# Opening loads reordered, first two units by halves, a wide form for gate and up, and new places for small vector work in a two-layer encoder trunk

## The reference, cut to what matters

```
x   : (1, 256, 1024)
# layer 0
h   = x @ e_w_in                       # 1024 x 2312: q, k, v of two head groups, forget gates
mix = concat(window_attention(h), forgetting_attention(h)) @ e_w_out
x   = layer_norm(ALPHA * x + mix)
x   = layer_norm(ALPHA * x + (silu(x @ w_gate) * (x @ w_up)) @ w_down)    # hidden width 2816
# layer 1
x   = layer_norm(ALPHA * x + differential_attention(x @ o_w_in) @ o_w_out)
logits = x @ w_router                  # 8 experts, top 2 of 8 for each token
x   = layer_norm(ALPHA * x + sum over the 2 chosen e of gate_e * expert_e(x))   # SwiGLU, hidden width 3584
```

## Time and profile before

| | |
|---|---|
| median of 3 runs | 1441.7 us (1440.79 to 1446.67) |
| the profiled execution | 1441.19 us, span 1439.4 us |
| TensorE busy | 1400.8 us, 97% of the span, 7602 matmuls |
| VectorE busy | 1114.2 us, 77% |
| ScalarE busy | 942.6 us, 65% |
| granted TensorE clock | 0.994 |
| read from HBM | 431.54 MB, 304 GB/s over the span |

### The profile page before, as it was taken

How to read it: one execution, slowest core, us unless ns; L and a number is a source line. 1 busy time by engine, 2 the same in 40 slices (tenths; PEclk the granted TensorE clock), 3 DMA queues, 4 the chain that set the end, 5 groups by cost and what they waited for, 6 DMA issues and landing times.

```text
span 1439.4 us, 19952 instructions
## 1 busy us (share of the span) xinstructions
PE 1400.8 (97%) x7602; PEld 1205.1 (84%) x7602; DVE 1114.2 (77%) x980; ACT 942.6 (65%) x837; POOL 36.7 (3%) x29
## 2 busy tenths in 40 slices
PE   8999999999989999999999999999999999999986
PEld 8988999989978888888888888888888888888865
DVE  4646544565567888988888888888888888889977
ACT  4655434345554777777777777777777777778755
POOL 1000000000000000000000000000000000000200
PEclk9999999999999999999999999999999999999999
DMA  9515545544146999999999999999999999999950
GB/s 364 222 64 215 190 176 189 191 147 176 60 180 260 415 422 379 366 390 386 352 400 382 356 382 386 372 371 385 376 361 411 373 357 389 385 378 374 370 202 31
DMA packets 62789, 438.59 MB, mean 305 GB/s; under 512 B 7096, under 2 KB 7120, under 8 KB 11152
## 3 DMA queue, kind: packets, MB, share of 16 engines
q1 hardware_dynamic: 59904, 425.75, 76.6%
q0 software_dynamic: 2688, 11.85, 2.3%
q10 hardware_dynamic: 144, 0.27, 0.1%
HBM read 431.54 MB, written 6.30 MB: 304 GB/s over the span
## 4 chain that ended last, share of the span: by engine, by line
PE 90%; DVE 4%; ACT 2%; DMA 2%; issue 1%; POOL 0%; SPq 0%; DVEq 0%; POOLq 0%; ACTq 0%
PE ps L503 29%; PE ps L505 28%; PE ps L504 28%; PE ps L873 2%; DMA work<-y_rows,mx 1%; ACT raw L1007 1%; DMA raw<-w_dense 1%; DVE raw L1266 1%; DVE wlo L1238 1%; PE ps L661 1%; PE ps L609 1%; PE ps L510 1%; PE ps L831 0%; DVE raw L1307 0%; DVE biasb L1484 0%
## 5 line engine op out<-in xcount | busy, mean ns | idle before, releaser
L1238 DVE TENSOR_TENSOR wlo<-raw,whi 128x2048 fp32r<-128x2048 f32 x398 | 909.8, 2291 | 203.4 <-ACT whi L957 201.7
L957 ACT ACTIVATE whi<-raw 128x2048 fp32r<-128x2048 f32 x398 | 762.1, 1918 | 274.3 <-PE ps L505 271.9
L503 PE MATMUL ps<-whi,xth 128*128 128x512 f32 (+1 forms) x1144 | 440.8, 385 | 3.3 <-ACT xth L972 1.6
L505 PE MATMUL ps<-whi,xtl 128*128 128x512 f32 (+1 forms) x1144 | 434.3, 380 | 0.0
L504 PE MATMUL ps<-wlo,xth 128*128 128x512 f32 (+1 forms) x1144 | 433.6, 379 | 0.0
L503 PEld LDWEIGHTS ps<-whi,xth 128*128 128x128 f32 x1144 | 215.3, 188 | 46.1 <-DVE wlo L1238 2.6
L505 PEld LDWEIGHTS ps<-whi,xtl 128*128 128x128 f32 x1144 | 215.2, 188 | 41.3
L504 PEld LDWEIGHTS ps<-wlo,xth 128*128 128x128 f32 x1144 | 215.5, 188 | 38.4
L503 PE MATMUL ps<-whi,hth 128*128 128x512 f32 x464 | 183.3, 395 | 7.1 <-DVE wlo L1238 7.1
L504 PE MATMUL ps<-wlo,hth 128*128 128x512 f32 x464 | 181.4, 391 | 0.0
L505 PE MATMUL ps<-whi,htl 128*128 128x512 f32 x464 | 181.4, 391 | 0.0
(11 more groups left out here) (234 smaller groups left out, 678.6 us busy)
## 6 DMA issues: line engine op xcount, KB each, us to landing
raw<-w_moe SPq DMA_DIRECT2D x336, 1024.0 KB, 7.1
raw<-w_dense SPq DMA_DIRECT2D x62, 1024.0 KB, 4.8
raw<-vec_rows POOLq DMA_DIRECT2D x4, 1024.0 KB, 6.1
y_rows<-work SPq DMA_DIRECT2D x8, 512.0 KB, 8.7
x<-x_in SPq DMA_DIRECT2D x2, 512.0 KB, 5.2
raw<-w_dense SPq DMA_DIRECT2D x2, 512.0 KB, 10.0
raw<-cum_rows POOLq DMA_DIRECT2D x1, 1024.0 KB, 9.9
x_rows<-x SPq DMA_DIRECT2D x2, 512.0 KB, 3.0
```

The source lines that it names most:

```text
L503: mm(o, lh, rh, start=start, stop=False)
L505: return mm(o, ll, rh, start=False, stop=stop)
L957: A(unit(whi, j), raw[:, slot * UNIT:(slot + 1) * UNIT], ACT.Copy).then_inc(hi_rdy, 1)
L1238: dve.tensor_tensor(unit(wlo, j), raw[:, slot * UNIT:(slot + 1) * UNIT], unit(whi, j).bitcast(F32), ALU.subtract).then_inc(lo_rdy, 1)
```

## The change

1. SP loads x block 0, first half of unit 0, x block 1, second half of unit 0, then unit 1 in two halves.
2. TensorE transposes only block 0 before unit 0. `first_cols` runs unit 0 by halves: k-tiles 0 to 3 for block 0, then the transposes of block 1, k-tiles 0 to 3 for block 1, then k-tiles 4 to 7 for both. `second_rows` runs unit 1 by halves. ScalarE and VectorE split units 0 and 1 by halves, ScalarE with the eviction of block 1 between the halves of unit 0.
3. `xth` and `xtl` become one tile `xt` with both parts of a k-tile side by side. `to_rows_wide` replaces `to_rows` for gate and up units: high weights times both parts in one matmul of 512 columns, low weights times the high part in one of 256, into a bank for each block. ScalarE copies the second half of each bank to SBUF, VectorE adds the first half to it; silu and product then work from SBUF. Gate uses banks 0 and 1, up banks 2 and 3, without alternation, and TensorE waits for the sum of the chunk before.
4. In `even_end` the evictions and the head output of group 3 stand ahead of the split of unit 12.
5. Ten warm matmuls in the routing become four.
6. `ROWS_AT` and `PICK_AT` have new values.

```diff
-WARM_ROUTE = (8, 8, 10, 3, 8)
+WARM_ROUTE = (8, 8, 4, 3, 8)
-PICK_AT = (24, 27, 30, 33)
-ROWS_AT = (1, 3, 6, 8, 12, 14, 18)
+PICK_AT = (26, 29, 32, 35)
+ROWS_AT = (0, 2, 4, 6, 8, 10, 12)
-        xth = sb("xth", [P, KT, TOK], F32R)
-        xtl = sb("xtl", [P, KT, TOK], F32R)
+        xt = sb("xt", [P, KT, 2, TOK], F32R)
+        xth, xtl = xt[:, :, 0, :], xt[:, :, 1, :]
+        gate_sum = htmp[:, :].rearrange("p (k n) -> p k n", k=2)
+        up_sum = work[:, 256:768].rearrange("p (k n) -> p k n", k=2)
...
-            for tb in range(TB):
-                sp.dma_start(x[:, tb, :], x_in[0, tb * P:(tb + 1) * P, :]).then_inc(x_here[tb], 16)
-            sp.dma_start(raw[:, 0:UNIT // 2], w_dense[0][:, 0:UNIT // 2]).then_inc(first_in, 16)
+            sp.dma_start(x[:, 0, :], x_in[0, 0:P, :]).then_inc(x_here[0], 16)
+            sp.dma_start(raw[:, 0:UNIT // 2], w_dense[0][:, 0:UNIT // 2]).then_inc(first_in[0], 16)
+            sp.dma_start(x[:, 1, :], x_in[0, P:2 * P, :]).then_inc(x_here[1], 16)
             sp.dma_start(raw[:, UNIT // 2:UNIT], w_dense[0][:, UNIT // 2:UNIT]).then_inc(loaded[0], 16)
-            for k in range(1, N_DENSE):
+            sp.dma_start(raw[:, UNIT:UNIT + UNIT // 2], w_dense[1][:, 0:UNIT // 2]).then_inc(first_in[1], 16)
+            sp.dma_start(raw[:, UNIT + UNIT // 2:2 * UNIT], w_dense[1][:, UNIT // 2:UNIT]).then_inc(loaded[1], 16)
+            for k in range(2, N_DENSE):
...
+            def to_rows_wide(k, bank):
+
+                h, l = as_cols(whi, k), as_cols(wlo, k)
+                for b in range(2):
+                    for kt in range(KT):
+                        c = slice(b * P, b * P + P)
+                        mm(ps[bank + b][:, :], h[:, kt, c], xt[:, kt, :, :], start=kt == 0, stop=False)
+                        r = mm(ps[bank + b][:, 0:TOK], l[:, kt, c], xth[:, kt, :], start=False, stop=kt == KT - 1)
+                return r
+
+            def first_cols():
+
+                h, l = as_cols(whi, 0), as_cols(wlo, 0)
+                pe.wait_ge(first_lo, 1)
+                for half in range(2):
+                    if half == 1:
+                        pe.wait_ge(lo_rdy, 1)
+                    for tb in range(TB):
+                        if half == 0 and tb == 1:
+                            turn(0, (2, 3))
+                        for kt in range(4 * half, 4 * half + 4):
+                            t = slice(tb * P, tb * P + P)
+                            r = three(ps[4][:, tb * 256:tb * 256 + 256], xth[:, kt, t], xtl[:, kt, t],
+                                      h[:, kt, :], l[:, kt, :], tb == 0 and kt == 0, tb == 1 and kt == KT - 1)
+                return r
...
-            turn(0)
+            turn(0, (0, 1))
...
-                    if what == "gate" and c >= 2:
-                        pe.wait_ge(f_h, c - 1)
-                    r = to_rows(k, (0 if what == "gate" else 2) + c % 2)
+                    if c:
+                        pe.wait_ge(f_gate if what == "gate" else f_up, c)
+                    r = to_rows_wide(k, 0 if what == "gate" else 2)
...
                 exps(3)
+                probs_out(3)
                 split(U_IN_E - 1 + SPLIT_AHEAD)
-                probs_out(3)
...
-            turned(0)
-            act.wait_ge(first_in, 16)
+            turned(0, (0, 1))
+            act.wait_ge(first_in[0], 16)
             A(whi[:, 0, 0:UNIT // 2], raw[:, 0:UNIT // 2], ACT.Copy).then_inc(first_hi, 1)
+            turned(0, (2, 3))
             act.wait_ge(loaded[0], 16)
             A(whi[:, 0, UNIT // 2:UNIT], raw[:, UNIT // 2:UNIT], ACT.Copy).then_inc(hi_rdy, 1)
...
+                    if what == "gate":
+                        act.wait_ge(w_used, k + 1)
+                        if c:
+                            act.wait_ge(f_lo, c)
+                        for b in range(2):
+                            A(gate_sum[:, b, :], ps[b][:, TOK:], ACT.Copy).then_inc(f_part, 1)
+                        act.wait_ge(f_gate, c + 1)
+                        A(htmp[:, :], htmp[:, :], ACT.Silu).then_inc(f_silu, 1)
                     if what == "up":
                         act.wait_ge(w_used, k + 1)
                         if c:
-                            act.wait_ge(f_lo, c)
-                        A(htmp[:, :], ps[c % 2][:, :], ACT.Silu).then_inc(f_silu, 1)
+                            act.wait_ge(f_h, c)
+                        for b in range(2):
+                            A(up_sum[:, b, :], ps[2 + b][:, TOK:], ACT.Copy).then_inc(f_part, 1)
...
+                    if what != "down":
+                        n0, o, done = (0, gate_sum, f_gate) if what == "gate" else (2, up_sum, f_up)
+                        for b in range(2):
+                            dve.wait_ge(f_part, 4 * c + n0 + b + 1)
+                            r = dve.tensor_tensor(o[:, b, :], ps[n0 + b][:, 0:TOK], o[:, b, :], ALU.add)
+                        r.then_inc(done, 1)
                     if what == "up":
+                        dve.wait_ge(f_up, c + 1)
                         dve.wait_ge(f_silu, c + 1)
-                        dve.tensor_tensor(htmp[:, :], htmp[:, :], ps[2 + c % 2][:, :], ALU.mult).then_inc(f_h, 1)
+                        dve.tensor_tensor(gate_sum, gate_sum, up_sum, ALU.mult).then_inc(f_h, 1)
```

More of the change, by code:

```diff
@@ L195, in hidden @@
             if c < FC - 1:
-                return hth[:, :], htl[:, :]
-            return (t[:, 0:2, :].rearrange("p k n -> p (k n)") for t in (xth, xtl))
+                return [t[:, :].rearrange("p (k n) -> p k n", k=2) for t in (hth, htl)]
+            return xth[:, 0:2, :], xtl[:, 0:2, :]
         cum_t = biasb[0:8, 0, 0:TOK]
@@ L241, in trunk @@
         loaded = [sem(f"loaded{i}") for i in range(SLOTS)]
-        first_in = sem("first_half_unit_in")
-        first_hi = sem("first_half_unit_hi_ready")
-        first_lo = sem("first_half_unit_lo_ready")
+        first_in = [sem(f"first_half_of_unit{k}_in") for k in range(2)]
+        first_hi = sem("first_halves_of_units_hi_ready")
+        first_lo = sem("first_halves_of_units_lo_ready")
         c_in = sem("consts_in")
@@ L285, in trunk @@
         sum_rdy = sem("branch_sum_ready")
+        f_part = sem("ffn_low_part_copied")
+        f_gate = sem("ffn_gate_sum_ready")
+        f_up = sem("ffn_up_sum_ready")
         f_silu = sem("ffn_silu")
@@ L561, in to_cols, with second_rows @@
                                   h[:, kt, 0:n], l[:, kt, 0:n], kt == 0, kt == KT - 1)
+                return r
[12 more added lines that the diff above has]
+                                      h[:, kt, :], l[:, kt, :], tb == 0 and kt == 0, tb == 1 and kt == KT - 1)
+                return r
+            def second_rows():
+                h, l = as_cols(whi, 1), as_cols(wlo, 1)
+                pe.wait_ge(first_lo, 2)
+                for half in range(2):
+                    if half == 1:
+                        pe.wait_ge(lo_rdy, 2)
+                    for b in range(2):
+                        for kt in range(4 * half, 4 * half + 4):
+                            c = slice(b * P, b * P + P)
+                            r = three(ps[5][:, b * TOK:(b + 1) * TOK], h[:, kt, c], l[:, kt, c],
+                                      xth[:, kt, :], xtl[:, kt, :], b == 0 and kt == 0, b == 1 and kt == KT - 1)
                 return r
@@ L572, in project @@
                         pe.wait_ge(in_ev, seen + i - 1)
-                    if k == 0:
-                        pe.wait_ge(first_lo, 1)
-                    else:
+                    if k > 1:
                         pe.wait_ge(lo_rdy, k + 1)
-                    r = to_cols(k, 4 + i % 2, width) if width else to_rows(k, 4 + i % 2)
+                    r = first_cols() if k == 0 else second_rows() if k == 1 else to_cols(k, 4 + i % 2, width) if width else to_rows(k, 4 + i % 2)
                     r.then_inc(w_used, 1)
@@ L1104, in _ @@
                         act.wait_ge(f_h, n + 1)
-                        A(list(hidden(n))[0], htmp[:, :], ACT.Copy).then_inc(f_hi, 1)
+                        A(hidden(n)[0], gate_sum, ACT.Copy).then_inc(f_hi, 1)
                 if k == K_IN_O - 1:
@@ L1410, in _ @@
             dve.wait_ge(c_in, 16)
-            turned(0)
-            for part, ready, done in ((slice(0, UNIT // 2), first_hi, first_lo), (slice(UNIT // 2, UNIT), hi_rdy, lo_rdy)):
-                dve.wait_ge(ready, 1)
-                dve.tensor_tensor(wlo[:, 0, part], raw[:, part], whi[:, 0, part].bitcast(F32), ALU.subtract).then_inc(done, 1)
-            split(1)
+            for k in range(2):
+                for half, ready, done in ((0, first_hi, first_lo), (1, hi_rdy, lo_rdy)):
+                    if k == 0:
+                        turned(0, (2 * half, 2 * half + 1))
+                    part = slice(half * UNIT // 2, (half + 1) * UNIT // 2)
+                    dve.wait_ge(ready, k + 1)
+                    dve.tensor_tensor(wlo[:, k, part], raw[:, k * UNIT + part.start:k * UNIT + part.stop],
```

(1 more changed line is left out.)

16 lines of the change are left out of this document (9 added, 7 removed).

## The result

The changed kernel takes 1433.37 us (median of 5 runs, 1432.49 to 1434.15), the kernel before beside it 1441.74 (5 runs, 1440.79 to 1446.67). The ratio is 0.9924, 95% interval 0.9906 to 0.9941. So it is faster, by more than the 0.5% that a measurement tells from no change, but by 8 us in the medians (11 by the ratio) and not by 17: the forecast of 1424.1 and its range of 1420 to 1430 were wrong. The profiled execution took 1433.37 us as well (span 1431.6); against the profiled execution of before (1441.19) it is 7.8 us shorter.

A forecast was written before the change was run, and what follows sets the result against it. The prediction took TensorE's one queue, busy 1400.8 of 1439.4 us, as the bound. Its terms 1.1 + 4.2 + 1.4 + 1.5 + 8.9 = 17.1 us, off 1441.2, gave 1424.1 us, range 1420 to 1430.

The forecast's parts named there:

- feed-forward part: Gate and up units: 352 pairs at 0.347 instead of 0.360 us save 4.7, less 0.5 at the end: 4.2 us.
- routing: Warm matmuls before the first expert's gather: four instead of ten let it start sooner, 1.5 us; bounds 2.4 to -0.3.
- opening: Kernel start: half unit loaded before the second x block and units by halves let unit 0 finish 1.1 us sooner.
- last expert: Last expert: earlier row indices and later sums remove VectorE's wait for gathered rows and TensorE's stall, 8.9 us.
- even attention: End of the even attention: evicting the turned probabilities before the weight split starts the next transposes sooner, 1.4 us.
- A: Feed-forward: the wide form brings nothing, mixed widths cost 0.360 us a k-tile; 1428.8 us, chance 0.15.
- B: Opening and routing bring nothing: half unit lands no earlier, clock stays low through the gather; 1426.7 us, chance 0.12.
- C: Last expert: the gathers wait for something else and stay late, so its gain is lost; 1433.0 us, chance 0.03.
- D: Feed-forward: the pipeline drains at each change of width, costing 56 us more; 1480 us, chance 0.02.

The follow-up runs named there:

- u_last: Changed kernel with only PICK_AT and ROWS_AT put back to their old values: 1441.03 us, ratio 0.9972.
- p_only: Kernel before with only PICK_AT set to (27, 33, 39, 40): 1434.53 us against 1444.02, ratio 0.9936.
- flat: Changed kernel with the wide matmul's moving operand given as one run of 512 instead of 2 x 256: 1435.83 us, one execution.
- group: Changed kernel with all wide matmuls of a block first, then all narrow ones: 1428.58 us, one execution.
- late: Changed kernel with ROWS_AT back at its old values and PICK_AT at (27, 33, 39, 40): 1430.52 us, ratio 0.9904.
- again: The changed kernel run once more, unedited: 1433.57 us, ratio 0.9932.
- u_open: Changed kernel with both x blocks loaded first and transposed before unit 0 again, units still split by halves: 1432.85 us, ratio 0.9923.
- best1: Changed kernel with the edits of flat and late together: 1431.75 us, ratio 0.9922.
- fill: Changed kernel with warm matmuls put in the opening's gaps, ahead of the waits for the evictions of x blocks 0 and 1: 1432.84 us, ratio 0.9918.
- u_route: Changed kernel with ten warm matmuls in the routing again instead of four: 1434.48 us, ratio 0.9928.
- nf10: As nf, but with ten warm matmuls in the routing instead of four: 1430.11 us, ratio 0.9907.
- nf: As best1, plus warm matmuls in TensorE's gaps in the opening, the odd layer and ahead of the routing's first choice: 1430.89 us, ratio 0.9899.

## Why the prediction was wrong, step by step

Of 1433.4 - 1424.1 = 9.3 us the feed-forward part misses 2.7, the routing 2.0, the opening 1.6, the odd layer 1.5, the last expert 1.35 and the even attention 0.1. Some 4.6 of them are TensorE's clock (1.3 in the opening, 1.5 in the odd layer, 1.8 in the routing): the forecast had no fall in the first two and only the short one of before in the third. These shares are read from two profiles; only the last expert was also shown by medians (u_last, p_only). No run puts the feed-forward form or the order in `even_end` back alone.

**Feed-forward, forecast 4.2, measured 1.5.** The step that failed is the sentence that reads a fixed 13.3 ns per instruction at both widths, so that the pair costs 0.347. It was read from long rows of one width and carried to alternating widths, where the pair took 0.3533. Of the 4.7 us, 352 x (0.3600 - 0.3533) = 2.4 came. The down units between lost 240 x (0.2294 - 0.2278) = 0.4, on which the forecast had no term, and the end of the part cost 0.58, forecast 0.5. That leaves 1.4 of the 1.5 measured. Why the pair costs 6 ns more stays open: flat excludes the form of the operand, group shows that 4 of them go when the widths don't alternate, and one program shows both 0.347 and 0.353 in its first two chunks.

**Last expert, forecast 8.9, measured 7.55.** The mechanism was right: u_last and p_only give the stall back and take it away alone. The size was off in the cost of the moved work, forecast 0.3 for two sums and nothing for the row steps. The two chunks with sums cost 0.67 each, the row steps 0.46: 9.18 for the stall and 0.17 for the chunk behind it, less 1.34 and 0.46, is 7.55. late, without these costs, gained the 1.9 back. It is the place and not the number of the sums: in the kernel before two sums share a chunk as well (units 30 and 33), and it takes 16.98 us, 0.17 over; with the sums at 32 and 35, the one at 32 right behind a product (0.68 and 1.28 in one go) and ahead of a split, it takes 17.47. What makes the one place dear is argued and not shown: that the product had used up half of the split's slack fits, but before, the sum at unit 30 stands just so behind a subtraction of 0.68 (1395.73, 1396.34).

**Routing, forecast 1.5, measured -0.5.** Within the stage TensorE got to the gather 1.3 us sooner, forecast 1.56; the sentence "if the clock rises as it did" is the one that failed, for the gather then took 1.8 us longer. The bound was a loss of 0.3 for 17 of 32 matmuls at double time; the fall lasted longer than that. All ten profiles with four warm matmuls show 6.83 us of low clock there, all four with ten show 3.41. Where the longer one begins differs: where it begins 6.0 to 6.6 us behind the first router matmul, the stage up to the first expert matmul takes 18.05 to 18.18 us (again, u_open, best1); where it begins 9.0 to 9.3 us behind, 19.08 to 19.26 (the changed kernel, u_last, flat, group, late, fill). With ten it took 18.65 to 18.67 each time (before, u_route, p_only, nf10). The mean of the nine with four is 18.82, and nf, with three more ahead of the first choice, took 18.73; so no gain or loss of this number can be told. Theory W, that the 0.38 us of idle time behind the four makes the low stretch longer, is refuted: in again, u_open, best1 and nf TensorE has no such idle time, and the stretch is 6.83 us there too. Why four go with the longer one stays open.

**Opening, forecast 1.1, measured -0.49 in this profile and +0.8 in the next of the same program.** The transfers were as read from the earlier trace rows. The forecast took TensorE's clock for granted because it was full there in the one profile of before; in p_only, whose opening is that of before, it was low from 9.7 for 6.8 us, and the eviction of unit 0 stands at 20.77 in place of 19.88. So a low clock in the opening does not come of the change.

**Even attention, forecast 1.4, measured 1.29.** Right; the third tile starts 1.35 us behind the first, the sum had 1.19 (97.56 to 98.75): the eviction begins 0.15 us after the transposes' end.

**The odd layer, not in the forecast, -1.48.** The clock fell at 323.0 in the profile after and not in the one of before. It is the fall and not the change: from its first matmul to the first router matmul the layer takes 119.4 us in the three profiles without a fall there and without added fillers (before, u_route, group) and 120.8 to 121.0 in the nine with one, and p_only, the same program as before up to the last expert, has the fall too (at 327.1). The forecast rested on one execution of before that was among its fastest: its profile shows two falls ahead of the last 7 us, while the program's later medians were 1445.17 (17 runs), 1444.29 (11) and 1444.02 (9), 1441.2 being their lowest. Had the sum been made against these, 17.1 us less would be 1427 to 1428, and the changed kernel run again was 11.6 us below the median beside it (9.8 by the ratio), not 7.8.

**The rivals.** A came at half its price: the pair took 0.353, between the forecast's 0.347 and A's 0.360, and whether by its mechanism is not shown. B happened: in the routing for the reason it gave, the clock, in the opening for the clock too and not for a late transfer. C and D did not happen.

## What to carry to other kernels

Ask of a stall first whether the waiting instruction can stand later in its queue: one constant was worth 9 us, and the rest of a large change 4. Price a sum that is put ahead of a split at that very unit, with what already stands beside it, and not against the chunk's total: two sums cost 0.67 us at one pair of places and 0.17 at another. A per-instruction price read from a long row of one width need not hold where widths alternate. Before a short stretch of rows is taken as the effect of an edit, look at the same stretch in several profiles without the edit, and at the whole part: flat's 0.3469 looked like a repair and stands in the unedited kernel too. Where the clock moves between executions, take the time from many of them and not from one profile.

## What was not expected of the hardware

**One program, two spacings.** At a full clock the pair of 512 and 256 columns took 0.347 us or 0.353, by the profile, in the first two of eleven chunks, and 0.353 in the other nine each time. The whole feed-forward part takes 192.4 us with the low value and 192.8 without, where no fall of the clock is in it. What decides between them is not shown; the form of the operand (2 x 256 or one run of 512) does not. In a row of their like (group) the wide ones are 0.231 apart.

**The clock falls at places that change from one execution to the next.** In 14 profiles, one of each program and two of the changed one, it was low for 3.4 us at a time around 8 to 10 (4 profiles, in p_only for 6.8), 64 to 66 (5), 128 to 133 (5), 321 to 327 (9), at 416 (nf) and in the routing (all 14, for 3.4 or 6.8). It was low for 6.8 us from 1376 in u_last and from 1378 in before, beginning within their stalls of 7 us, and in the last 6 to 10 us of every profile. Most of these places lie at a wait of TensorE or a few us behind one: 1.78 us ahead of 322.75 in the changed kernel, 1.62 ahead of 415.57 in nf. Over 17 executions of the kernel before, the time grew by 0.37 us for each us of low clock (worked out as twice the share that its granted clock misses of full, times the span; correlation 0.94; the 11 and the 9 executions beside the later runs give 0.47 and 0.29), and their times ran from 1441.28 to 1449.45. A fall of 3.4 us in the middle of dense matmuls costs about 1.5 us, as at 323 (119.4 us for the odd layer without it, 120.9 with it).

The Trainium skill, page "TensorE: Matmul & The Clock Gate", section "What's actually happening", says that the number of matmuls run at the low clock differs between runs of one kernel and should not be fitted to a fixed count. These traces agree: 14 warm records in the opening took 2.86 us in one profile of the changed kernel and 1.80 in the next.
